# Head pairs and the dense experts' last norm of a one-layer decoder step: sums and spread moved between matmul groups, norm ahead of receptance, residual added on TensorE and moments taken by ScalarE

## Chip, core and metric

The kernel runs on one core of a Trainium2 chip, as one program. The time is the device time of one execution in microseconds (us), median over runs.

## The reference, cut to what matters

One layer of a decoder over 1024 prompt tokens and 8 single-token samples: an input projection, window attention beside an RWKV-7 time mix, a merge with layer norm, and a retrieval over 16,384 one-neuron experts with a second layer norm. The change touches two places. In the time mix:

```
kk = hs(k * k_k)                                                   # per head of 64
kk = kk * lax.rsqrt(jnp.maximum(jnp.sum(kk * kk, -1, keepdims=True), 1e-24))
k = k * (1.0 + (a - 1.0) * k_a)
bonus = (jnp.sum(hs(r * k * r_k), -1, keepdims=True) * hs(v))
```

And in the last step, where `peer` is the expert sum and `layer_norm` takes mean and mean squared deviation over 1024 features with an epsilon of 1e-5:

```
y = layer_norm(DEEPNORM_ALPHA * h + peer(h, ...), ln2_g, ln2_b)
```

## The kernel before

The trunk runs twice. The early part (`e_` tiles) holds 256 prompt tokens and the 8 samples, 264 columns in one column group (`NG` = 1). The late part (`l_` tiles) holds 768 tokens in two column groups of 384 (`NG` = 2). In each part `project_pairs` loops over the 8 pairs of heads. The engines run their own programs in program order and meet at semaphores whose counts come from the three lists `PE`, `AC` and `DV` (`Steps`). Layout: features of a pair on the 128 partitions, tokens along the free axis.

A turn of the loop (pair p) on TensorE: the two small products w and a (L776), g (L776), the projection r (L770, 8 weight tiles for each column group), the sums of squares per head (L797, one 128-token run after another, into `sums`), the projection v, the spread of the reciprocal norm over 64 partitions (L805, into `rb`), the bonus product (L776, of `rk`), in the early part three transposes (L813), the projection k of the next pair, and in the early part six more transposes (L825, `dec_t`). All three projections write the same PSUM tile `zp[0]`, so v waits until ScalarE has copied r out, and k until v is out. w of the next pair waits for `bonus_done`, since the bonus product and w share `zp[1]`; g waits until ScalarE has made tanh of w (L856).

On VectorE a turn is: fk, kkr, sq (the squares), the decay and its scan, ta and kp, a block of background work, the clamp (L969), fr and rk (L947, L973), the reciprocal (L977), kk and kka (L980, L981), a second background block, fv and bonus (L947, L991), the four products alpha, beta, kappa, rho (L995), dend, betae and kappae (L998), and in the early part two copies of the transposes (L1003, L1004).

The background work (`Rows`, `bg.dve`) is there in the late part only: GpSimd fetches expert rows by index into a ring, VectorE takes dot products (L440), adds weighted rows (L457) and does selection steps. `beside["pair"]` gives each block 4 slots (four dots, or four adds with a selection step) in pairs 0, 2, 4 and 6, 8 slots in pairs 1, 3 and 5, none in pair 7. ScalarE copies and scales each projection, then takes the square root of the clamped norm and the exponentials, and at the end of a turn applies Gelu to the dots. SyncE loads weights and stores results; in a turn it stores the gate, fv and the bonus, then the six products. An early turn and a late turn are numbered 0 to 7 below.

`experts` is the last stage. Three blocks of 128 tokens (`ND` = 3) go densely through all experts in 16 chunks of 8 tiles: TensorE makes 8 tiles of scores (L2755, from `l_c_wo`, loaded as `u_cols`), ScalarE Gelu (L2773), VectorE the gate weight (L2796), and TensorE the 48 matmuls into `vps` (L2763). Beside it the rows of three more blocks are fetched and added by VectorE. After the last chunk and the last row, VectorE adds ALPHA times h to `vps` (L2812), takes moments (L465 to L467), and normalises (L472 to L474).

Of the kernel before, what the change touches and what calls it, by code (L numbers as in the profile page):

```python
# [14 lines left out]
P = 128  # L15
# [629 lines left out]
def project_pairs(nc, A, pt, bg, plan):  # L645
# [6 lines left out]
    PE = Steps("w", "a", "g", "r", "ss", "v", "rb", "bonus", *only("raw_t", "dec_t"))  # L652
    AC = Steps("w", "a", "g", "r", "r_s", "norm", "Dinv", "D", "Dprev", *only("wdec"), "v", "v_s", *only("raw_t"))
    DV = Steps("k_f", *only("k_fs"), "kkr", "sq", "lw", "scan", "lprev", "a", "ka1", "kp",
               "ssm", "r_f", *only("r_fs"), "rk", "rinv", "kk", "kka", "v_f", *only("v_fs"),
               "alpha", "beta", "kappa", "rho", "dend", "betae", "kappae", *only("dec_t0", "dec_t1"))
# [7 lines left out]
    with ExitStack() as ctx:  # L664
# [52 lines left out]
        def _(sp):  # L717
# [12 lines left out]
            def store(p):  # L730
# [3 lines left out]
                sp.wait_ge(dve_done, DV.after("v_f", p))  # L734
                sp.dma_start(A["rw"][p, R_V, :, tokens], fv[:, PROMPT]).then_inc(rw_out[R_V], 16)
                sp.wait_ge(bonus_done, p + 1)
                for here, there in pt.spans:
                    sp.dma_start(A["bonus"][p, :, there], bonus[:, here]).then_inc(b_out, 16)
                for name, i in (("alpha", R_ALPHA), ("beta", R_BETA), ("kappa", R_KAPPA), ("rho", R_RHO),
# [3 lines left out]
                    if name == "rho":  # L743
                        sp.wait_ge(dve_done, DV.after("dend", p))
                        sp.dma_start(A["dend"][p, :, pt.t0 // CL:pt.t0 // CL + NC], dend[:, :]).then_inc(d_out, 16)

# [19 lines left out]
        def _(pe):  # L766
            def project(q, s, done):
                for g in range(NG):
                    for k in range(KT):
                        mm = pe.matmul(zp[s][:, g, 0:GZ], w[q][:, k, :], xT[:, k, g * GZ:(g + 1) * GZ],  # L770
                                       start=(k == 0), stop=(k == KT - 1))
                mm.then_inc(done, 1)

# [8 lines left out]
            for p in range(NPAIR):  # L782
# [11 lines left out]
                project(Q_PAIR_R, 0, pe_done)  # L794
                pe.wait_ge(dve_done, DV.after("sq", p))
                for i, (o, m) in enumerate(runs):
                    mm = pe.matmul(sums[0:m, 2 * i:2 * i + 2], sq[:, o:o + m], bd[:, 0:P:HD], start=True, stop=True)  # L797
                mm.then_inc(pe_done, 1)
                pe.wait_ge(w_in[2], 16 * p + 16)
                pe.wait_ge(act_done, AC.after("r", p))  # L800
                project(Q_PAIR_V, 0, pe_done)
                pe.wait_ge(dve_done, DV.after("rinv", p))
                for i, (o, m) in enumerate(runs):
                    for h in range(2):
# [2215 lines left out]
```

## Time and profile before

| | |
|---|---|
| median of 3 runs | 4436.56 us (4434.66 to 4444.74) |
| profiled execution, its own time | 4439.95 us |
| span of the profile | 4438.0 us |
| TensorE busy | 3811.5 us (86%) |
| VectorE busy | 3042.0 us (69%) |
| ScalarE busy | 949.5 us (21%) |

The profile is one execution. A row of the timeline has the start in us from the span's start, the duration in us, engine, line, operation, output and inputs, shapes and the count of merged instructions; brackets hold the idle time of that engine just ahead and what ended it. One fp32 matmul of the source shows as two records. A busy share says little here, as each stage has its own limit: what counts is which wait ends last in the stage that changes.

### The profile page before, as it was taken

Reading aid. Unit: us, or ns where it says so; the run is one execution under the profiler, and the core shown is the slowest. Engines: PE = TensorE matmul, PEld = TensorE weight load, DVE = VectorE, ACT = ScalarE, POOL = GpSimd, SP = SyncE. Lnnn points to the kernel's source line nnn. Section 1 sums busy time; section 2 is a strip of 40 time slices with the busy share of each in tenths; the row PEclk is TensorE's granted clock in tenths of the full one; section 3 lists DMA queues with packets and bytes.
Section 4 is the critical chain, followed back from the end, with each engine's and each line's share of the span. In section 5 each row is a group of like instructions: output and inputs, shape, how many; then the busy total and the mean of one; then the engine's idle time right before and its main releaser. Section 6 shows DMA issues by size and latency. Waiting matters only on the chain. (4 is left out here: it accounts for less than half of the span.)

```text
span 4438.0 us, 71873 instructions
## 1 busy us (share of the span) xinstructions
PE 3811.5 (86%) x28123; PEld 2546.5 (57%) x28123; DVE 3042.0 (69%) x5972; ACT 949.5 (21%) x1985; POOL 1818.0 (41%) x1489
## 2 busy tenths in 40 slices
PE   7986788799988788888778886669999999999997
PEld 6766665555555477777665464554544444445443
DVE  0454432588588557777686478877888888977768
ACT  1341220110233222222351013770000000010000
POOL 0016000067133023333225207736666566666664
PEclk9997889899998898898679997669999999999998
DMA  7542353499576556765639643449999999999997
GB/s 172 162 155 91 111 182 142 151 360 403 188 258 233 198 197 215 249 219 188 212 125 381 244 157 48 99 145 404 407 398 393 405 403 398 384 405 407 404 406 285
DMA packets 434557, 1152.50 MB, mean 260 GB/s; under 512 B 80735, under 2 KB 175524, under 8 KB 430852
## 3 DMA queue, kind: packets, MB, share of 16 engines
q0 software_dynamic: 207216, 687.87, 42.8%
q1 hardware_dynamic: 194276, 419.98, 26.1%
q10 hardware_dynamic: 32727, 40.05, 2.6%
q8 instruction: 224, 3.67, 0.3%
q14 instruction: 114, 0.93, 0.1%
HBM read 1044.67 MB, written 113.65 MB: 261 GB/s over the span
## 5 line engine op out<-in xcount | busy, mean ns | idle before, releaser
L2755 PE MATMUL x_sps<-c_big,l_c_wo 128*128 128x384 f32 x2048 | 689.8, 499 | 80.1 <-DMA l_c_wo<-u_cols 70.1
L384 POOL DMA_INDIRECT l_w_ring<-u_rows,k_eidx x256 | 295.3, 1153 | 967.0 <-DVE l_w_dots L440 410.3
L2763 PE MATMUL x_vps<-l_c_v,x_w 128*128 128x512 f32 x1536 | 662.1, 592 | 1.6 <-DVE x_w L2796 1.6
L384 POOL DMA_INDIRECT w_ring<-u_rows,k_eidx x384 | 483.3, 1259 | 429.3 <-DVE w_dots L440 254.5
L2755 PEld LDWEIGHTS x_sps<-c_big,l_c_wo 128*128 128x128 f32 x2048 | 399.3, 196 | 371.1 <-DMA l_c_wo<-u_cols 78.1
L457 DVE SCALAR_TENSOR_TENSOR w_yacc<-w_ring,w_wts,w_yacc 128x1024 f32<-128x1024 f32 x384 | 493.4, 1285 | 63.3 <-DMA w_ring<-v_rows,k_eidx 49.1
L2763 PEld LDWEIGHTS x_vps<-l_c_v,x_w 128*128 128x128 f32 x1536 | 291.8, 190 | 365.9 <-issue 358.2
L440 DVE CUSTOM_DVE_ANT_0 w_ring<-w_ring,w_h 128x1024 f32<-128x1024 f32 x384 | 452.5, 1224 | 49.7 <-DMA w_h<-s_h 25.9
L384 POOL DMA_INDIRECT w_ring<-v_rows,k_eidx x384 | 423.6, 1103 | 130.5 <-issue 114.8
L384 POOL DMA_INDIRECT l_w_ring<-v_rows,k_eidx x256 | 290.2, 1133 | 316.7 <-DVE l_w_yacc L457 253.0
L457 DVE SCALAR_TENSOR_TENSOR l_w_yacc<-l_w_ring,l_w_wts,l_w_yacc 128x1024 f32<-128x1024 f32 x256 | 328.9, 1285 | 30.7 <-DMA l_w_ring<-v_rows,k_eidx 18.8
L580 PE MATMUL l_pzp<-c_big,l_c_w 128*128 128x384 f32 x960 | 313.0, 488 | 18.0 <-DMA l_c_w<-w_tiles 18.0
L440 DVE CUSTOM_DVE_ANT_0 l_w_ring<-l_w_ring,l_w_h 128x1024 f32<-128x1024 f32 x256 | 305.6, 1224 | 20.4 <-DMA l_w_ring<-u_rows,k_eidx 9.7
L2773 ACT ACTIVATE x_w<-x_sps 128x384 f32<-128x384 f32 x128 | 62.7, 490 | 1139.5 <-PE x_sps L2755 984.5
L580 PEld LDWEIGHTS l_pzp<-c_big,l_c_w 128*128 128x128 f32 x960 | 182.4, 190 | 148.2 <-DMA l_c_w<-w_tiles 18.3
L770 PE MATMUL l_qzp<-c_big,l_c_w 128*128 128x385 f32 x768 | 260.9, 498 | 4.2 <-PEq L144 4.2
L2370 POOL DMA_INDIRECT s_G<-l_f_at_gate,l_f_at_u x128 | 207.4, 1620 | 125.6 <-DVEq L2553 67.9
L770 PEld LDWEIGHTS l_qzp<-c_big,l_c_w 128*128 128x128 f32 x768 | 149.1, 195 | 111.8 <-issue 15.8
L2796 DVE TENSOR_TENSOR x_w<-x_w,l_c_wo 128x384 f32<-128x384 f32 x128 | 68.1, 558 | 154.1 <-ACT x_w L2773 151.9
L2320 PE MATMUL l_f_gps<-l_f_two,l_f_one 128*128 128x128 f32 x512 | 101.9, 361 | 75.0 <-ACT l_f_two L2428 67.2
L2320 PEld LDWEIGHTS l_f_gps<-l_f_two,l_f_one 128*128 128x128 f32 x512 | 87.9, 259 | 87.7 <-ACT l_f_two L2428 73.5
L580 PE MATMUL e_pzp<-c_big,e_c_w 128*128 128x264 f32 x480 | 116.8, 402 | 19.7 <-DMA e_c_w<-w_tiles 12.7
(642 smaller groups left out, 6170.1 us busy)
## 6 DMA issues: line engine op xcount, KB each, us to landing
l_c_wo<-u_cols SPq DMA_DIRECT2D x128, 512.0 KB
l_c_v<-v_rows SPq DMA_DIRECT2D x128, 512.0 KB
e_c_w<-w_tiles SPq DMA_DIRECT2D x54, 512.0 KB, 3.5
l_c_w<-w_tiles SPq DMA_DIRECT2D x54, 512.0 KB
l_c_wo<-s_G SPq DMA_DIRECT2D x16, 1536.0 KB
s_rw<-l_q_out SPq DMA_DIRECT2D x48, 384.0 KB
s_G<-l_f_stage ACTq DMA_DIRECT2D x8, 2048.0 KB
s_zT<-l_pz ACTq DMA_DIRECT2D x30, 384.0 KB
```

The source lines that it names most:

```text
L384: pool.indirect_dma_start(out=self.ring[:, r, :], out_offset=None, in_=self.A[table], in_offset=bass.IndirectOffsetOnAxis(ap=idx[:, s:s + ...
L440: V.tensor_tensor_reduce(ring[:, q % self.RING, :], ring[:, q % self.RING, :], self.h[b % self.HB][:, :], 1.0, 0.0, ALU.mult, ALU.add, sel ...
L457: self.mark(dve, V.scalar_tensor_tensor(ya[:, :], self.ring[:, q % self.RING, :], self.wts[:, s:s + 1], ya[:, :], ALU.mult, ALU.add), self ...
L580: mm = pe.matmul(zp[j][:, g, 0:GN], w[u % 3][:, k, :], xT[:, k, x0 + g * GN:x0 + (g + 1) * GN], start=(k == 0), stop=(k == KT - 1))
L770: mm = pe.matmul(zp[s][:, g, 0:GZ], w[q][:, k, :], xT[:, k, g * GZ:(g + 1) * GZ], start=(k == 0), stop=(k == KT - 1))
L2320: mm = pe.matmul(gps[q % 2][:, t * NKEY:(t + 1) * NKEY], one[q % 2][:, t, :], two[q % 2][:, t, :], start=True, stop=True)
L2370: pool.indirect_dma_start(out=matrix, out_offset=bass.IndirectOffsetOnAxis(ap=at_u[:, s:s + 1], axis=0), in_=gates[:, s:s + 1], in_offset= ...
L2755: mm = pe.matmul(sps[n % 2][:, 0:ND * P], u[n % 4][:, k, :], hT[:, k, :], start=(k == 0), stop=(k == KT - 1))
L2763: mm = pe.matmul(vps[k][:, x * 512:(x + 1) * 512], w[:, e, k * P:(k + 1) * P], v[:, e, x * 512:(x + 1) * 512], start=(c == 0 and e == 0), ...
L2773: act.activation(w[:, e, :], sps[n % 2][:, 0:ND * P], ACT.Gelu).then_inc(S["act_done"], 1)
L2796: V.tensor_tensor(w[:, e, :].rearrange("p (g t) -> p g t", t=TGW), w[:, e, :].rearrange("p (g t) -> p g t", t=TGW), G[:, :, e, :], ALU.mul ...
```

## The change

In `project_pairs` the orders change. With one column group the sums of squares stand ahead of projection r and the spread stays behind projection v. With two groups the sums stand between the two column groups of r and the spread between those of v. The clamp moves directly behind kp, ahead of the first background block, and the reciprocal directly behind that block, ahead of fr and rk; ScalarE's square root moves ahead of the copy of r. On VectorE the products alpha to kappae move ahead of fv and the bonus, and the second background block moves behind the bonus. The stores of fv and bonus move behind the six products in SyncE's program.

In `experts` six fp32 matmuls of ALPHA times the identity with h are put into the accumulation of `vps`, in the middle of the scores of the last chunk. VectorE's sum and moments are gone; ScalarE copies `vps` with a running sum, scales it to the negative mean, squares the deviation with a running sum and takes the root, for blocks 0 and 1 ahead of the last row block's own square root and for block 2 behind it.

```
-    PE = Steps("w", "a", "g", "r", "ss", "v", "rb", "bonus", *only("raw_t", "dec_t"))
+    PE = Steps("w", "a", "g", "ss", "r", *(("rb", "v") if pt.ng > 1 else ("v", "rb")), "bonus", *only("raw_t", "dec_t"))
...
-            def project(q, s, done):
+            def project(q, s, done, between=None):
+
                 for g in range(NG):
...
+                    if between is not None and g == 0 < NG - 1:
+                        between()
                 mm.then_inc(done, 1)
+                if between is not None and NG == 1:
+                    between()
+
+            def squares(p):
+                pe.wait_ge(dve_done, DV.after("sq", p))
...
+            def spread(p):
+                pe.wait_ge(dve_done, DV.after("rinv", p))
...
-                project(Q_PAIR_R, 0, pe_done)
-                pe.wait_ge(dve_done, DV.after("sq", p))
...
+                if NG == 1:
+                    squares(p)
+                project(Q_PAIR_R, 0, pe_done, None if NG == 1 else lambda: squares(p))
                 pe.wait_ge(w_in[2], 16 * p + 16)
                 pe.wait_ge(act_done, AC.after("r", p))
-                project(Q_PAIR_V, 0, pe_done)
-                pe.wait_ge(dve_done, DV.after("rinv", p))
...
+                project(Q_PAIR_V, 0, pe_done, lambda: spread(p))
                 pe.wait_ge(act_done, AC.after("g", p))
+                pe.wait_ge(dve_done, DV.after("rk", p))
                 small(1, bd[:, :], rk[:, :])
...
                 act.activation(pt.grouped(gate[:, :]), zp[1][:, :, 0:GN], ACT.Copy).then_inc(act_done, 1)
+                act.wait_ge(dve_done, DV.after("ssm", p))
...
                 do("kp", V.scalar_tensor_tensor(kp[:, :], kp[:, :], 1.0, fk[:, :], ALU.add, ALU.mult))
-                bg.dve(dve, 4 * fetched(p))
                 dve.wait_ge(pe_done, PE.after("ss", p))
...
                 do("ssm", ins)
...
+                bg.dve(dve, 4 * fetched(p))
                 dve.wait_ge(act_done, AC.after("norm", p))
...
                 do("kka", V.tensor_tensor(kka[:, :], kk[:, :], ta[:, :], ALU.mult))
-                bg.dve(dve, 4 * fetched(p))
-                dve.wait_ge(act_done, AC.after("v_s", p))
+                dve.wait_ge(act_done, AC.after("Dprev", p))
...
+                dve.wait_ge(act_done, AC.after("v_s", p))
+                mixed(2, fv, "v", C_MUV)
...
+                bg.dve(dve, 4 * fetched(p))
```

The last stage:

```
+                    if (c, e) == (NCH - 1, CH // 2):
+                        pe.wait_ge(S["ident_done"], 1)
+                        pe.wait_ge(S["acc_in"], 16 * ND)
+                        for k in range(ND):
+                            for x in range(2):
+                                pe.matmul(vps[k][:, x * 512:(x + 1) * 512], scaled_ident[:, :], acc[:, k, x * 512:(x + 1) * 512],
+                                          start=False, stop=False)
...
+            def moments(k):
+
+                one = slice(k, k + 1)
+                act.wait_ge(S["v_psum"], ND * (NCH - 1) + k + 1)
+                act.activation(acc[:, k, :], vps[k][:, :], ACT.Copy, accum_out=nm3[:, one]).then_inc(S["moments"], 1)
...
+                act.activation(nm3[:, one], nm3[:, one], ACT.Copy, scale=-1.0 / DM).then_inc(S["moments"], 1)
...
+                act.activation(u[k][:, :, :].rearrange("p a b -> p (a b)"), acc[:, k, :], ACT.Square, bias=nm3[:, one],
+                               accum_out=ss3[:, one]).then_inc(S["moments"], 1)
...
+                act.activation(rs3[:, one], ss3[:, one], ACT.Sqrt, bias=eps[:, :], scale=1.0 / DM).then_inc(S["std3"], 1)
...
+            rows.act(act, rows.NGT + 1 - rows.act_at)
+            act.wait_ge(S["eps_done"], 1)
+            for k in range(ND - 1):
+                moments(k)
             rows.act(act, rows.TOTAL)
...
+            moments(ND - 1)
...
-            dve.wait_ge(S["acc_in"], 16 * ND)
             for k in range(ND):
-                dve.wait_ge(S["v_psum"], ND * (NCH - 1) + k + 1)
-                mark(V.scalar_tensor_tensor(acc[:, k, :], acc[:, k, :], ALPHA, vps[k][:, :], ALU.mult, ALU.add), S["summed"], k + 1)
...
+                dve.wait_ge(S["std3"], k + 1)
+                lnk(V.reciprocal(rs3[:, one], rs3[:, one]))
```

TensorE's program in an early turn before the change: `e_qsums` are the sums of squares, `e_qrb` the spread, and the 8-row products into `e_qzp` are the projections r and v.

```order
L776 MATMUL e_qzp<-e_q_lora,e_q_up 128x264 x3
L770 MATMUL e_qzp<-c_big,e_c_w 128x264 x8
L797 MATMUL e_qsums<-c_bd,e_q_sq 128x2 x2
L797 MATMUL e_qsums<-c_bd,e_q_sq 8x2
L770 MATMUL e_qzp<-c_big,e_c_w 128x264 x8
L805 MATMUL e_qrb<-c_ident,e_q_norm 64x128 x4
```

The same place after the change:

```order
L795 MATMUL e_qzp<-e_q_lora,e_q_up 128x264 x3
L782 MATMUL e_qsums<-c_bd,e_q_sq 128x2 x2
L782 MATMUL e_qsums<-c_bd,e_q_sq 8x2
L771 MATMUL e_qzp<-c_big,e_c_w 128x264 x16
L789 MATMUL e_qrb<-c_ident,e_q_norm 64x128 x4
```

The sums of squares stood between the projections r and v; now they stand ahead of r, and r and v follow each other with nothing between.

TensorE's program in a late turn before the change, from w, a and g to the next pair's k:

```order
L776 MATMUL l_qzp<-l_q_lora,l_q_up 128x384 x6
L770 MATMUL l_qzp<-c_big,l_c_w 128x385 x16
L797 MATMUL l_qsums<-c_bd,l_q_sq 128x2 x6
L770 MATMUL l_qzp<-c_big,l_c_w 128x385 x16
L805 MATMUL l_qrb<-c_ident,l_q_norm 64x128 x12
L776 MATMUL l_qzp<-l_q_fk,c_bd 128x384 x2
L770 MATMUL l_qzp<-c_big,l_c_w 128x385 x16
```

And after it:

```order
L795 MATMUL l_qzp<-l_q_lora,l_q_up 128x384 x6
L771 MATMUL l_qzp<-c_big,l_c_w 128x385 x8
L782 MATMUL l_qsums<-c_bd,l_q_sq 128x2 x6
L771 MATMUL l_qzp<-c_big,l_c_w 128x385 x16
L789 MATMUL l_qrb<-c_ident,l_q_norm 64x128 x12
L771 MATMUL l_qzp<-c_big,l_c_w 128x385 x8
L795 MATMUL l_qzp<-l_q_fk,c_bd 128x384 x2
L771 MATMUL l_qzp<-c_big,l_c_w 128x385 x16
```

The sums moved into the middle of r and the spread into the middle of v; the second group of r and the first of v now stand side by side.

VectorE's program in an early turn before the change, from kka (L981) on: fv, bonus, the products, the two copies.

```order
L981 TENSOR_TENSOR e_q_ta<-e_q_kk,e_q_ta 128x264
L947 SCALAR_TENSOR_TENSOR e_q_fv<-e_qz,e_q_prm,e_q_fv 128x256
L949 SCALAR_TENSOR_TENSOR e_q_fv<-e_q_sh,e_q_prm,e_q_fv 128x8
L991 TENSOR_TENSOR e_q_bonus<-e_qzp,e_q_fv 128x264
L995 TENSOR_TENSOR e_q_out<-e_q_kk,e_q_lprev 128x256
L995 TENSOR_TENSOR e_q_out<-e_q_ta,e_q_Di 128x256
L995 TENSOR_TENSOR e_q_out<-e_q_kp,e_q_Di 128x256
L995 TENSOR_TENSOR e_q_out<-e_q_fr,e_q_lcum 128x256
L996 COPY e_q_dend<-e_q_lcum 128x4
L998 TENSOR_TENSOR e_q_out<-e_q_out,e_q_dend 128x256 x2
L1003 COPY e_q_decn<-e_qtp 8x512
```

And after it:

```order
L992 TENSOR_TENSOR e_q_ta<-e_q_kk,e_q_ta 128x264
L1000 TENSOR_TENSOR e_q_out<-e_q_kk,e_q_lprev 128x256
L1000 TENSOR_TENSOR e_q_out<-e_q_ta,e_q_Di 128x256
L1000 TENSOR_TENSOR e_q_out<-e_q_kp,e_q_Di 128x256
L1000 TENSOR_TENSOR e_q_out<-e_q_fr,e_q_lcum 128x256
L1001 COPY e_q_dend<-e_q_lcum 128x4
L1003 TENSOR_TENSOR e_q_out<-e_q_out,e_q_dend 128x256 x2
L959 SCALAR_TENSOR_TENSOR e_q_fv<-e_qz,e_q_prm,e_q_fv 128x256
L961 SCALAR_TENSOR_TENSOR e_q_fv<-e_q_sh,e_q_prm,e_q_fv 128x8
L1009 TENSOR_TENSOR e_q_bonus<-e_qzp,e_q_fv 128x264
L1015 COPY e_q_decn<-e_qtp 8x512
```

fv and the bonus moved behind the seven products and dend; the late turn has the same order, with the second background block behind the bonus.

## Rows read from the trace of the kernel before

**Rows 1.** Page, 40 slices: busy tenths of the DMA engines

```profile
DMA  7542353499576556765639643449999999999997
```

**Rows 2.** Timeline, an early turn, TensorE

```profile
194.94 3.72 PE L770 MATMUL e_qzp<-c_big,e_c_w 128*128 128x264 f32 x16
...
198.50 0.63 PE L797 MATMUL e_qsums<-c_bd,e_q_sq 128*128 128x2 f32 x6
...
199.24 3.80 PE L770 MATMUL e_qzp<-c_big,e_c_w 128*128 128x264 f32 x16
...
202.97 0.87 PE L805 MATMUL e_qrb<-c_ident,e_q_norm 128*64 128x128 f32 x12
...
208.21 0.27 PE L825 MATMUL e_qtp<-c_ident,e_q_fr 128*8 128x128 f32 x1
```

**Rows 3.** Timeline, the same turn, VectorE

```profile
193.28 0.68 DVE L1003 COPY e_q_decn<-e_qtp 8x512 f32<-8x512 f32 x1 [0.15 <-PE e_qtp L825]
...
195.61 0.43 DVE L955 TENSOR_TENSOR e_q_sq<-e_q_kkr 128x264 f32<-128x264 f32 x1
...
205.70 0.43 DVE L991 TENSOR_TENSOR e_q_bonus<-e_qzp,e_q_fv 128x264 f32<-128x264 f32 x1
...
208.08 0.88 DVE L998 TENSOR_TENSOR e_q_out<-e_q_out,e_q_dend 128x256 f32<-128x256 f32 x2
...
209.12 0.68 DVE L1003 COPY e_q_decn<-e_qtp 8x512 f32<-8x512 f32 x1 [0.15 <-PE e_qtp L825]
```

**Rows 4.** Timeline, late turns, TensorE

```profile
1161.22 6.58 PE L776 MATMUL l_qzp<-l_q_lora,l_q_up 64*128 64x384 f32 x12 [2.01 <-issue]
...
1207.95 1.56 PE L776 MATMUL l_qzp<-l_q_lora,l_q_up 128*128 128x384 f32 x4 [1.81 <-ACT l_q_tw L856]
...
1254.23 2.94 PE L776 MATMUL l_qzp<-l_q_lora,l_q_up 64*128 64x384 f32 x8 [5.44 <-DVE l_q_bonus L991]
...
1259.51 10.51 PE L770 MATMUL l_qzp<-c_big,l_c_w 128*128 128x385 f32 x32
...
1271.12 10.60 PE L770 MATMUL l_qzp<-c_big,l_c_w 128*128 128x385 f32 x32
...
1284.50 10.51 PE L770 MATMUL l_qzp<-c_big,l_c_w 128*128 128x385 f32 x32
1297.62 2.16 PE L776 MATMUL l_qzp<-l_q_lora,l_q_up 64*128 64x384 f32 x8 [2.61 <-DVE l_q_bonus L991]
1300.69 2.93 PE L776 MATMUL l_qzp<-l_q_lora,l_q_up 128*128 128x384 f32 x4 [0.91 <-ACT l_q_tw L856]
```

**Rows 5.** Timeline, late turns, ScalarE

```profile
1203.71 0.81 ACT L845 ACTIVATE l_qz<-l_qzp 128x770 f32<-128x770 f32 x1 [11.43 <-PE l_qzp L770]
...
1205.61 1.28 ACT L394 ACT_TABLE_LOAD   x1
```

**Rows 6.** Timeline, late turns, VectorE

```profile
1218.50 1.22 DVE L440 CUSTOM_DVE_ANT_0 l_w_ring<-l_w_ring,l_w_h 128x1024 f32<-128x1024 f32 x1
...
1231.43 0.17 DVE L969 TENSOR_SCALAR l_q_norm<-l_qsums 128x12 f32<-128x12 f32 x1
...
1524.36 1.95 DVE L998 TENSOR_TENSOR l_q_out<-l_q_out,l_q_dend 128x768 f32<-128x768 f32 x2
```

**Rows 7.** Timeline, last chunk of the experts stage, TensorE

```profile
4321.47 20.80 PE L2755 MATMUL x_sps<-c_big,l_c_wo 128*128 128x384 f32 x64
...
4348.30 23.42 PE L2755 MATMUL x_sps<-c_big,l_c_wo 128*128 128x384 f32 x64 [6.03 <-DMA l_c_wo<-u_cols]
4371.55 41.36 PE L2763 MATMUL x_vps<-l_c_v,x_w 128*128 128x512 f32 x96
```

**Rows 8.** Timeline, last chunk and end, VectorE

```profile
4361.95 0.56 DVE L2796 TENSOR_TENSOR x_w<-x_w,l_c_wo 128x384 f32<-128x384 f32 x1 [3.75 <-ACT x_w L2773]
...
4415.01 1.22 DVE L2812 SCALAR_TENSOR_TENSOR x_acc<-x_acc,x_vps 128x1024 f32<-128x1024 f32 x1
...
4424.44 0.16 DVE L472 RECIPROCAL x_rs<-x_rs 128x1 f32<-128x1 f32 x1
```

More of the change, by code:

```diff
@@ L745, in store @@
                         sp.dma_start(A["dend"][p, :, pt.t0 // CL:pt.t0 // CL + NC], dend[:, :]).then_inc(d_out, 16)
+                sp.wait_ge(dve_done, DV.after("v_f", p))
+                sp.dma_start(A["rw"][p, R_V, :, tokens], fv[:, PROMPT]).then_inc(rw_out[R_V], 16)
+                sp.wait_ge(bonus_done, p + 1)
+                for here, there in pt.spans:
+                    sp.dma_start(A["bonus"][p, :, there], bonus[:, here]).then_inc(b_out, 16)
             load_up(0)
@@ L771, in project @@
                                        start=(k == 0), stop=(k == KT - 1))
+                    if between is not None and g == 0 < NG - 1:
+                        between()
                 mm.then_inc(done, 1)
+                if between is not None and NG == 1:
+                    between()
+            def squares(p):
+                pe.wait_ge(dve_done, DV.after("sq", p))
+                for i, (o, m) in enumerate(runs):
+                    mm = pe.matmul(sums[0:m, 2 * i:2 * i + 2], sq[:, o:o + m], bd[:, 0:P:HD], start=True, stop=True)
+                mm.then_inc(pe_done, 1)
+            def spread(p):
+                pe.wait_ge(dve_done, DV.after("rinv", p))
+                for i, (o, m) in enumerate(runs):
+                    for h in range(2):
+                        mm = pe.matmul(rb[h * HD:(h + 1) * HD, o // GN, o % GN:o % GN + m], norm[0:m, 2 * i + h:2 * i + h + 1].broadcast_to([m, HD]),
+                                       ident[0:m, 0:m], start=True, stop=True)
+                mm.then_inc(pe_done, 1)
             def small(s, lhsT, rhs):
@@ L864, in _ @@
                 act.activation(pt.grouped(gate[:, :]), zp[1][:, :, 0:GN], ACT.Copy).then_inc(act_done, 1)
+                act.wait_ge(dve_done, DV.after("ssm", p))
+                for i, (rows, cols) in enumerate(whole):
+                    ins = act.activation(norm[rows, cols], norm[rows, cols], ACT.Sqrt)
+                ins.then_inc(act_done, 1)
                 act.wait_ge(pe_done, PE.after("r", p))
@@ L874, in _ @@
                     shift(Q_PAIR_R, p)
-                act.wait_ge(dve_done, DV.after("ssm", p))
-                for i, (rows, cols) in enumerate(whole):
-                    ins = act.activation(norm[rows, cols], norm[rows, cols], ACT.Sqrt)
-                ins.then_inc(act_done, 1)
                 act.activation(Di[:, :], lcum[:, :], ACT.Exp, scale=-1.0).then_inc(act_done, 1)
@@ L2808, in _ @@
             rows.dve(dve, 8 * rows.TOTAL)
[L2809 removed]
             for k in range(ND):
[L2811 to L2815 removed]
+                one = slice(k, k + 1)
+                dve.wait_ge(S["std3"], k + 1)
+                lnk(V.reciprocal(rs3[:, one], rs3[:, one]))
+                lnk(V.scalar_tensor_tensor(acc[:, k, :], acc[:, k, :], nm3[:, one], rows.ln[:, 0, :], ALU.add, ALU.mult))
+                mark(V.scalar_tensor_tensor(acc[:, k, :], acc[:, k, :], rs3[:, one], rows.ln[:, 1, :], ALU.mult, ALU.add),
+                     S["acc_done"], k + 1)
 def program(nc, A, phases=99):
```

49 lines of the change are left out of this document (18 added, 31 removed).

## The prediction

> **What bounds the kernel now.** I read the page first, then the timeline of the stages that change, engine by engine, then the waits there. On the page the reader is to see the DMA engines full through the last nine slices but the very end [rows 1]: in the experts stage the loads set the pace, so time gained ahead of it shifts it whole, and only its last 60 us can be won inside it. The change touches three stages, each with its own limit, and the sum is one term for each.
>
> Early turns (one column group). TensorE is nearly always at work. A turn lasts 209.12 - 193.28 = 15.84 us [rows 3]. The sums (0.63 us) run between r and v, and v starts at 199.24, a tenth of a microsecond after they end: in that time ScalarE copies r out of PSUM, so the sums cost nothing there [rows 2].
>
> Late turns (two groups). TensorE and VectorE hold each other up. TensorE waits 5.44 us and 2.61 us at the start of a turn for the bonus, which VectorE makes only after its second background block [rows 4]. The stage lasts from 1161.22 [rows 4] to 1524.36 + 1.95 = 1526.31 [rows 6], 365.1 us.
>
> The end. VectorE starts the dense tail at 4415.01 and reaches the first reciprocal at 4424.44 [rows 8]. TensorE is done at 4371.55 + 41.36 = 4412.9 [rows 7]. So the last thing that bounds is VectorE's own queue.
>
> **Early turns: a loss.** The sums now stand ahead of r and wait for sq. In the rows sq ends at 195.61 + 0.43 = 196.04 [rows 3], while r began at 194.94 [rows 2]. VectorE cannot be earlier: sq is behind the two copies, and these wait for TensorE's transposes. So TensorE waits until about 196.15, does the sums (0.63 us, some 0.1 more since its weight loads are no longer hidden), and starts r at 196.9: 1.9 us late. From r to v nothing is won back, since ScalarE's copy, not the sums, sets the 4.30 us between their starts. Second, the transposes of `dec_t` wait for fv, now behind the products. VectorE's products end at 208.08 + 0.88 = 208.96; with the bonus (0.4) moved behind fv, fv ends near 208.6 and the transposes start near 208.8 in place of 208.21 [rows 2, 3]: 0.55 us. A turn gets 15.84 + 1.9 + 0.55 = 18.3 us. Seven full turns give 7 x 2.45 = 17, the first wait is half as long since VectorE has no copies ahead of it, and the last turn keeps only the 0.55: together **+18.5 us**. Bounds: +13 (the wait halved, as if sq came 0.8 us sooner) and +22 (all weight loads of the sums exposed and a semaphore's delay at each of three hand-overs). The square root ahead of the copy of r costs nothing here, as the clamp is free before r's 3.6 us end; if it were late, v would be.
>
> **Late turns: a gain.** With the second background block behind the bonus, w never waits, if VectorE gets kk to bonus done within the projection k. The new turn on TensorE, from the end of one k to the next:
> - to the start of g: 4.35 us. In the turn at 1203.6 (ScalarE's copy begins at 1203.71) g starts at 1207.95, held by tanh, which stands behind the copy, the scaling, a table load of 1.28 and a Gelu [rows 4, 5];
> - g, then r with the sums in the middle: 1.39 (taken off the start of r at 1259.51 and the row of g, 1.56 with overlap) and 1271.12 - 1259.51 = 11.61 [rows 4];
> - new: v waits for the copy of r, no longer covered by the sums: 0.81 [rows 5] and two hand-overs, 1.2 us;
> - v with the spread, and the bonus product: 1284.50 - 1271.12 = 13.38 [rows 4]; k: 10.5 [rows 4].
>
> That is 42.4 us. The background blocks that stay on this path: the first one now stands between clamp and reciprocal, and the spread needs the reciprocal 23.8 us into the turn. In pairs 1, 3 and 5 the block is two groups long, 1231.43 - 1218.50 = 12.93 us [rows 6]. The clamp comes when the sums are done, at 12.4, so the reciprocal is there at 25.7: a wait of 1.9 us, and another 1.3 for a spread at the lower clock, 45.7 us. Pair 3 has a block some 2 us longer by its selection steps (my estimate), 47.6; pair 5 a shorter one, no wait. In the one-group pairs the reciprocal is there in time. After a two-group turn VectorE starts its next turn 6 to 8 us late, which moves kp and with it clamp and root to 14 to 16.5, just ahead of the end of r at 17.4: if that were more, ScalarE's copy of r would be queued behind the root, and v behind it.
>
> Sum: turn 0 takes 43.4, turns 1 and 3 45.7 and 47.6, four turns 42.4, and the last ends with VectorE's bonus near 37.7 (it has no k): 344. Against 365.1 this is **-21 us**. Bounds: -7 (next part) and -30 (no wait and no gap at all).
>
> **A rule on ScalarE's table loads.** The row shows 1.28 us for the load, and g started 1207.95 - 1205.61 = 2.34 us after the load did [rows 4, 5]. A tanh of 768 columns, which by the copy's row takes 0.8 to 0.9, and a Gelu of four columns are in these 2.34, so nothing else is. The Trainium skill, page "ScalarE: Activation LUTs", section "What ACT_TABLE_LOAD costs", gives each switch a drain of about 1.38 us on top. By that an estimate from the page would put 1.4 us more into each of seven late turns and the late gain at 11 us instead of 21; the rows show no such drain, so I go by them.
>
> **The end: a gain.** VectorE loses L2812 to L467 for three blocks: 4424.44 - 4415.01 = 9.43 us [rows 8]. It keeps the reciprocal and two passes for each. ScalarE's new work is four steps of at most 1.1 us for each block (770 columns take 0.81 [rows 5], so 1024 take near 1.05): the third block starts when TensorE is done and is ready 3 us later, 4416; VectorE needs it 5.7 us after its start. TensorE's six extra matmuls cost 41.36 / 48 x 6 = 5.2 us [rows 7] and are put where it waits 6.03 us for a tile of `u_cols` [rows 7]: hidden. If that wait were gone they would put TensorE 5.2 us later and cost VectorE some 3. They may give more: behind the wait, four tiles took 23.42 us, where the four ahead took 20.80 [rows 7], so a busy TensorE saves 2.6, and VectorE waits 3.75 us for ScalarE in that stretch [rows 8]. The end gives **-12 us**, between -6 and -12.5.
>
> The other pieces cost nothing: the scaled identity and epsilon are made at the stage's start; h is loaded as before; in SyncE's program the store of fv and bonus moves behind six stores, and all are issued before the next pair's k is done.
>
> **Sum.** +18.5 - 21 - 12 = -14.5 on 4439.95 us of the profiled execution, which stands 3.4 above the median. On the median: 4422, and with a little of the clock case below, **4423**.
>
> **The rivals.**
> - *The clock drops in the late turns.* A wait of 1.8 us ahead of g left it at full rate (1.56), but after 2.61 + 0.91 us of idle g took 2.93 us [rows 4], which is 1.2 in place of 2.4 GHz. The new turn idles 1.8 ahead of g and 1.2 ahead of v, on either side of that. If each of six turns loses the 1.4 us in g and near 1 us in the first matmuls of r (my estimate), the late gain is 7, and the total -0.5: 4436. The Trainium skill, page "TensorE: Matmul & The Clock Gate", section "Why this matters for your kernels", warns of idle gaps between bursts of matmuls for this reason. Chance 0.2.
> - *Slower: the early turns lose the clock as well.* TensorE now idles twice in a turn of 18 us, 1.1 ahead of the sums and 0.7 ahead of v. If all of r (3.6 us) ran at half rate in each turn, 8 x 3.6 = 29 us are added: 4452. It ends above no change from about 3 us a turn. For it speaks the row at 2.93, against it that today's early turns idle about as often, in shorter pieces. Chance 0.1.
> - *The late turns gain their whole idle time*, as the copies out of PSUM overlap better than I have them: -30, total 4413. Chance 0.1.
> - *The extra matmuls do not fit the wait*, because the tile lands sooner: the end gives 6, total 4428. Chance 0.1.
>
> **How the numbers follow.** My forecast has 0.5, with its own range of 4416 to 4430. A measurement of this kernel tells about 0.2% (9 us) from no change, so faster means below 4427.7. Of the forecast 0.45 lies there, all of the third rival and half of the fourth: 0.6. Same gets 0.3, slower 0.1. The range 4408 to 4442 leaves out most of the second rival and the fringes.
>
> **What would show it.** In the profile after: early turns of 18.3 us with TensorE waiting for sq ahead of L782, and the pause between r and v still 0.7; late turns of 42 to 43 us without a wait for the bonus, 2 to 4 us of wait for the reciprocal in pairs 1 and 3 only; six L2768 matmuls inside the wait near 4342 and no wait of 6 us left; VectorE going from the last row's norm straight into reciprocals without a stall. The prediction is wrong if early turns stay at 16 us, if late turns show g near 2.9 throughout, or if VectorE waits for ScalarE at the end.

## The result, and the profile after the change

The changed kernel takes 4448.13 us (median of 20 runs, 4431.67 to 4464.11) against 4435.87 us for the kernel before (20 runs, 4427.53 to 4444.74): the ratio is 1.0027, with a 95% interval of 1.0017 to 1.0037. It is slower by some 12 us, where a gain of 12 to 14 us (4423) was forecast. The profiled execution after has 4456.54 us and a span of 4454.7.

The early turns, TensorE's timeline, to hold against [rows 2]:

```profile
199.64 0.71 PE L795 MATMUL e_qzp<-e_q_lora,e_q_up 128*128 128x264 f32 x2 [0.56 <-ACT e_q_tw L868]
201.38 0.70 PE L782 MATMUL e_qsums<-c_bd,e_q_sq 128*128 128x2 f32 x6 [1.03 <-DVE e_q_sq L967]
202.02 5.51 PE L771 MATMUL e_qzp<-c_big,e_c_w 128*128 128x264 f32 x16
208.10 3.80 PE L771 MATMUL e_qzp<-c_big,e_c_w 128*128 128x264 f32 x16 [0.57 <-ACT e_qz L882]
...
221.38 0.70 PE L782 MATMUL e_qsums<-c_bd,e_q_sq 128*128 128x2 f32 x6 [1.03 <-DVE e_q_sq L967]
222.01 3.83 PE L771 MATMUL e_qzp<-c_big,e_c_w 128*128 128x264 f32 x16
226.41 3.80 PE L771 MATMUL e_qzp<-c_big,e_c_w 128*128 128x264 f32 x16 [0.57 <-ACT e_qz L882]
...
240.32 5.49 PE L771 MATMUL e_qzp<-c_big,e_c_w 128*128 128x264 f32 x16
```

The wait for sq and the pause ahead of v are there as forecast. But r (16 records) takes 3.83 us in two of the seven full turns and 5.5 in the other five: from r at 222.01 to r at 240.32 are 18.31 us, the 18.3 of the forecast, and from r at 202.02 to r at 222.01 are 19.99. The granted clock tells them apart: as a share of 2.4 GHz it is 1.00 from 222.01 to 225.84 and 0.69 from 202.02 to 207.53, so a part of these matmuls ran at 1.2 GHz and the rest at 2.4. Before, r took 3.72 us in each full turn, as in [rows 2]. The windows of 165 to 293 us show it over the whole stretch, before and then after (busy time by engine, then PEclk, 0.98 and 0.93):

```profile
165.00:293.00 128.00, 115.01 (x635) 89.68 (x633) 86.88 (x238) 65.29 (x139) 13.51 (x24) 0.98 0.53 166
```

```profile
165.00:293.00 128.00, 112.18 (x548) 83.09 (x547) 71.42 (x193) 56.07 (x118) 10.42 (x19) 0.93 0.47 146
```

The late turns, TensorE after the change, from one w to the next, to hold against [rows 4]:

```profile
1228.93 2.53 PE L795 MATMUL l_qzp<-l_q_lora,l_q_up 64*128 64x384 f32 x8
1233.27 2.67 PE L795 MATMUL l_qzp<-l_q_lora,l_q_up 128*128 128x384 f32 x4 [1.81 <-ACT l_q_tw L868]
1235.73 5.97 PE L771 MATMUL l_qzp<-c_big,l_c_w 128*128 128x385 f32 x16
...
1249.21 5.41 PE L771 MATMUL l_qzp<-c_big,l_c_w 128*128 128x385 f32 x16 [0.99 <-ACT l_qz L882]
1256.47 1.53 PE L789 MATMUL l_qrb<-c_ident,l_q_norm 128*64 128x128 f32 x24 [1.84 <-issue]
...
1274.94 1.56 PE L795 MATMUL l_qzp<-l_q_lora,l_q_up 64*128 64x384 f32 x4
```

No turn waits for the bonus any more. The waits that are left up to the last turn are those forecast: 1.8 or 1.9 ahead of g, 1.0 ahead of v, and in pair 1 a wait of 1.84 ahead of the spread (3.6 in pair 3, as the run "late part and end" below shows in its own rows). What was not counted is g at 2.67 in place of 1.56, and the first half of r at 5.97 in place of 5.34: together 8.64 us in place of 6.90, and the other turns of this trace with a slow g have much the same, 8.55 to 8.64. Nor was a wait of 3.43 us ahead of g in the last turn, which the kernel before has too (3.44). From 1185.54 to VectorE's last bonus at 1536.4 the stage has 350.8 us, not 344, against 365.1.

The end, TensorE and then VectorE after the change, to hold against [rows 7, 8]:

```profile
4351.25 20.80 PE L2775 MATMUL x_sps<-c_big,l_c_wo 128*128 128x384 f32 x64
4371.89 5.31 PE L2768 MATMUL x_vps<-x_acc,x_scaled_ident 128*128 128x512 f32 x12
4377.04 20.80 PE L2775 MATMUL x_sps<-c_big,l_c_wo 128*128 128x384 f32 x64
4397.68 41.36 PE L2783 MATMUL x_vps<-l_c_v,x_w 128*128 128x512 f32 x96
```

```profile
4439.75 1.28 DVE L474 SCALAR_TENSOR_TENSOR w_yacc<-w_yacc,w_rs,w_ln 128x1024 f32<-128x1024 f32 x1
4441.07 0.17 DVE L2849 RECIPROCAL x_rs<-x_rs 128x1 f32<-128x1 f32 x1
4441.27 1.28 DVE L2850 SCALAR_TENSOR_TENSOR x_acc<-x_acc,x_nm,w_ln 128x1024 f32<-128x1024 f32 x1
```

The six extra matmuls are L2768. VectorE goes from the last row's norm into the first reciprocal without a stall. From its arrival at the dense tail to the end of the span are 4454.7 - 4441.07 = 13.6 us; before they were 4438.0 - 4415.01 = 23.0 [rows 8]. That is the forecast's 9.4, and in each of the nine traces with the new end these last steps take 13.6 us. TensorE shows no wait for `u_cols` here, so the six extra matmuls stand in the open with 5.3 us, but TensorE is done at 4439.0, ahead of VectorE.

### The profile page after: what moved, and what is told of

The parts are those of the page before. It is cut to its first block and busy times, and to the rows that moved or that the text cites. A ratio compares the mean times of both kernels' runs of the same rounds, so it can differ in the third digit from the quotient of the medians.

```text
span 4454.7 us, 71922 instructions
## 1 busy us (share of the span) xinstructions
PE 3838.5 (86%) x28135; PEld 2563.1 (58%) x28135; DVE 3034.9 (68%) x5958; ACT 958.4 (22%) x2001; POOL 1827.2 (41%) x1489
```

## Experiments

Each run is told with its ratio to the kernel before on the same chip. Chips differ (medians of before from 4404 to 4439 us), so only ratios and lengths of stages are compared. "Early part" is the stretch from the first matmul of the early pairs to the first of the scan behind them, "late part" the same for the late pairs, each from the starts that the traces show. Line numbers differ between the kernels.

### One part at a time

**The end alone.** `project_pairs` as before, the experts stage as changed.

> The kernel before with only the change at the end of the experts stage. By the theory read from the two traces the end gives what it gives in the changed kernel: from VectorE's arrival at the dense tail to the end of the span 13.6 us in place of 23.0, and the whole kernel about 9 to 12 us faster (ratio near 0.9975). Rival: the gain is given back ahead of the tail, because the six extra matmuls put TensorE later or the trace's 9.4 us was luck of one execution: then the time is within 4 us of before.

Measured: ratio 0.9991 (0.9980 to 1.0002). From VectorE's first dense reciprocal at 4377.39 to the end of the span (4391.0) again 13.6 us. The timing alone does not tell the gain from nothing. Over the traces of all kernels here, the first experts matmul to the end of the span took 1443.6 us in the mean of nine without the new end (1439.0 to 1448.1) and 1434.7 in nine with it (1429.4 to 1439.1): 8.9 us less.

**The pairs, in the early part alone and in the late part alone.** The experts stage is as before. Both forms of the function stand in the file, as `project_pairs_0` (before) and `project_pairs_1` (changed), and one is chosen by the number of column groups; for the late part alone the names are exchanged:

```
 def project_pairs(nc, A, pt, bg, plan):
+    one = project_pairs_1 if pt.ng == 1 else project_pairs_0
+    one(nc, A, pt, bg, plan)
```

> The kernel before with the pair change only where there is one column group (the early part). By the theory that the early turns lost 27 us in the changed kernel (exposed sums and the wait for v some 13, the wait for fv some 6, r at the lower clock some 9) the whole kernel is 25 to 30 us slower (ratio near 1.0061), the first e_r_ps matmul that reads e_c_powers is 27 us later, and what follows is shifted by the same amount with no growth. Rival: a loss at the start also costs the later stages (the changed kernel was a further 14 us later between the late turns and the last expert chunks): then 35 to 45 us slower. Second rival, my forecast's size of this term: 18.5 us slower.

Measured: 1.0068 (1.0048 to 1.0088), 30 us slower; the early part 178.3 us against 150.4 in the end-only kernel on that chip.

> The kernel before with the pair change only where there are two column groups (the late part). By the trace of the changed kernel the late turns give 14 us, so 14 us faster (ratio near 0.9968) if nothing behind them changes. Rival: the scan, attention and experts stages behind the late turns lose 12 to 14 us as a consequence of the late change (the trace of the changed kernel lost them there): then within 4 us of before. Second rival: the forecast's 21 us.

Measured: 0.9971 (0.9958 to 0.9985), 13 us faster; the late part 379.5 us against 390.9. It keeps its gain.

**Late part and end, early part as before.**

> The changed kernel with the early part as it was before: pair change in the late part, dense residual and statistics at the end. If the parts add up and the early part is what costs: 14 plus 9 to 12, so 23 to 26 us faster than before (ratio near 0.9945), faster than both kernels. If the later stages lose because of the late change: only 9 to 12 us faster. If the early part's 27 us were partly made up for by slack elsewhere, less than 12 + 27 = 39 us would lie between this and the changed kernel.

Measured: 0.9955 (0.9939 to 0.9971), 20 us faster. The three parts add up: +30 - 13 - 4 = +13, where the whole change has +12; each of the three has an interval of 5 to 9 us to either side. So the early part alone turned a gain into a loss. TensorE's rows of g and of the spread in the late turns of this kernel, each with the wait ahead of it in brackets, show the clock come and go:

```profile
1200.66 2.59 PE L1173 MATMUL l_qzp<-l_q_lora,l_q_up 128*128 128x384 f32 x4 [1.81 <-ACT l_q_tw L1246]
...
1223.86 1.53 PE L1167 MATMUL l_qrb<-c_ident,l_q_norm 128*64 128x128 f32 x24 [1.85 <-DVE l_q_norm L1363]
...
1246.77 1.56 PE L1173 MATMUL l_qzp<-l_q_lora,l_q_up 128*128 128x384 f32 x4 [1.91 <-ACT l_q_tw L1246]
...
1314.12 2.83 PE L1167 MATMUL l_qrb<-c_ident,l_q_norm 128*64 128x128 f32 x24 [3.61 <-DVE l_q_norm L1363]
...
1338.42 2.93 PE L1173 MATMUL l_qzp<-l_q_lora,l_q_up 128*128 128x384 f32 x4 [1.91 <-ACT l_q_tw L1246]
```

The same wait of 1.9 us is followed by g at 1.56 in one turn and at 2.93 in another.

### What costs in the early turns

All three have the early change alone, with one thing in it altered.

**fv and the bonus back ahead of the products.**

```
-               "alpha", "beta", ..., "kappae", "v_f", *only("v_fs"), ...
+               "v_f", *only("v_fs"), "alpha", "beta", ..., "kappae", ...
```

> The pair change in the early part only, with fv and the bonus back ahead of the products; the sums stay ahead of r and the products, clamp and root as in the change. By the theory that the dec_t transposes waited 0.7 to 0.9 us a turn for fv behind the products, the early part is 5 to 6 us shorter than with the whole early change, and the kernel some 24 us slower than before (with the early change alone it was 30 slower). Rival: dec_t was never what set the next turn, so the time stays at +30; or the next turn's sq gets later because VectorE has more ahead of it, and the waiting moves there. In the trace: no wait left ahead of the dec_t transposes.

Measured: 1.0055 (1.0037 to 1.0072), 24 us; early part 171.1, so 7 less than 178.3, of which 1.7 are one turn fewer with r at 5.51 (four of seven, not five). Both theories have something: the wait ahead of the `dec_t` transposes is gone in all turns but the last, and TensorE, earlier at the sums, waits a little longer there. One turn and the next:

```profile
181.30 0.70 PE L1160 MATMUL e_qsums<-c_bd,e_q_sq 128*128 128x2 f32 x6 [1.52 <-DVE e_q_sq L1345]
181.94 5.51 PE L1149 MATMUL e_qzp<-c_big,e_c_w 128*128 128x264 f32 x16
...
200.82 0.70 PE L1160 MATMUL e_qsums<-c_bd,e_q_sq 128*128 128x2 f32 x6 [1.08 <-DVE e_q_sq L1345]
201.45 3.83 PE L1149 MATMUL e_qzp<-c_big,e_c_w 128*128 128x264 f32 x16
```

**Sums and root back behind r.**

```
-                if NG == 1:
-                    squares(p)
-                project(Q_PAIR_R, 0, pe_done, ...)
+                project(Q_PAIR_R, 0, pe_done)
+                squares(p)
```

> The pair change in the early part only, with the sums back between r and v and the root back behind ScalarE's copy and scaling of r; fv stays behind the products. By the theory that the sums' place costs both the exposed wait for sq (some 13 us over the stage, with the wait ahead of v) and the drop of the clock in r (9 us in the trace of the changed kernel, 5.5 us in place of 3.7 in five of seven turns), only the 6 us of the dec_t wait are left: 6 to 8 us slower than before. Rival: the clock drops because of the longer wait ahead of the transposes and not because of the wait for sq: then r stays at 5.5 us in most turns and the kernel is 15 us slower.

Measured: 1.0003 (0.9987 to 1.0020), 3 us slower in the medians, which does not tell it from before; early part 155.8. The rival falls: with a wait of 0.37 still ahead of the transposes and 0.56 ahead of g, r is at full rate in each of the seven full turns.

```profile
193.22 0.27 PE L1214 MATMUL e_qtp<-c_ident,e_q_fr 128*8 128x128 f32 x1 [0.37 <-DVE e_q_fv L1338]
...
195.79 3.72 PE L1149 MATMUL e_qzp<-c_big,e_c_w 128*128 128x264 f32 x16
199.35 0.63 PE L1160 MATMUL e_qsums<-c_bd,e_q_sq 128*128 128x2 f32 x6
200.09 3.80 PE L1149 MATMUL e_qzp<-c_big,e_c_w 128*128 128x264 f32 x16
```

**The waits filled with work.**

```
+            def fill(count):
+                for _ in range(count):
+                    pe.matmul(dump[:, 0:256], bd[:, :], xT[:, 0, 0:256], start=True, stop=True)
...
+                    fill(3)
                     squares(p)
...
+                    fill(1)
                 pe.wait_ge(act_done, AC.after("r", p))
```

> The pair change in the early part only, with three matmuls of 256 columns into an unused bank of PSUM ahead of the wait for sq and one ahead of the wait for the copy of r in each turn, so that TensorE is busy in most of its two waits; nobody reads their result. If the idle time ahead of the sums is what takes the clock, r lasts 3.8 us in every turn and the kernel is 9 to 12 us faster than with the early change alone, some 20 slower than before. Rival: the clock follows something else (the 0.2 us matmuls of the sums and transposes, the mean load of the stage): r stays at 5.5 us in most turns, and the kernel is 30 us slower or more, since three matmuls at the lower clock (2.3 us) no longer fit the wait.

Measured: 1.0057 (1.0038 to 1.0076), 23 to 25 us slower, in place of 30; early part 168.7, which is 10 less than with the early change alone and 19.0 more than the mean of 149.7 in three traces of before. The times alone would not tell this from the early change; the length of the early part does. Order and waits are the same, only idle time ahead of the sums and of v was replaced, and r is back at 3.83 in every turn:

```profile
198.17 1.46 PE L1160 MATMUL e_qdump<-c_big,c_bd 128*128 128x256 f32 x6
199.46 0.63 PE L1165 MATMUL e_qsums<-c_bd,e_q_sq 128*128 128x2 f32 x6
200.02 3.83 PE L1150 MATMUL e_qzp<-c_big,e_c_w 128*128 128x264 f32 x16
203.68 0.59 PE L1160 MATMUL e_qdump<-c_big,c_bd 128*128 128x256 f32 x2
204.33 3.83 PE L1150 MATMUL e_qzp<-c_big,e_c_w 128*128 128x264 f32 x16
```

A turn has 218.29 - 200.02 = 18.27 us from r to r. The window of 165 to 293 us in this kernel has PEclk 1.00:

```profile
165.00:293.00 128.00, 120.75 (x638) 92.52 (x637) 79.18 (x212) 59.53 (x124) 11.84 (x21) 1.00 0.50 157
```

### What costs in the late turns

All three have the early part as before and the new end.

**The waits ahead of g and v filled.**

```
+                fill(4)
                 pe.wait_ge(act_done, AC.after("w", p))
                 small(1, up[:, 1, :], lora[1][:, :])
...
+                fill(2)
                 pe.wait_ge(act_done, AC.after("r", p))
```

> Late pair change and the end, early part as before (the e4 version), with four matmuls of 256 columns into an unused bank of PSUM ahead of TensorE's wait for the tanh of w and two ahead of its wait for the copy of r, in each late turn; nobody reads their result. In e4 five of the late turns ran g at 2.3 to 2.9 us in place of 1.56 and the first sixteen matmuls of r longer than 5.3. If the idle 1.8 to 1.9 us ahead of g take the clock, g is 1.6 in every turn, the stage from the first projection to the scan's first matmul falls from 379.4 to 370 us or less, and the kernel is 28 to 30 us faster than before. Rival: the clock falls for another reason (the load over a longer stretch, or the waits for the reciprocal in pairs 1 and 3), then g stays at 2.3 to 2.9 and the stage at 379, or longer, since four matmuls at half rate (3 us) do not fit the wait.

Measured: 0.9918 (0.9895 to 0.9941), 36 us faster than before; late part 370.8, which is 8.6 less than in the version without filling. The two timings lie 16 us apart, but they come from two chips and their intervals touch, so the other 7 are not shown to be a gain. g is 1.56 in each of the last seven turns, where the version without filling has 2.3 to 2.9 in five of them. The waits ahead of the spread are not filled: in pair 3 one of 3.76 us is still followed by matmuls at the lower clock, 6.80 us in place of 5.44. In the first turn TensorE has no wait ahead of g: there the four take 3.6 us, and the turn has 45.0 us in place of 43.5.

```profile
1205.75 1.99 PE L1160 MATMUL l_qdump<-c_big,c_bd 128*128 128x256 f32 x8
1207.63 1.56 PE L1178 MATMUL l_qzp<-l_q_lora,l_q_up 128*128 128x384 f32 x4
1209.02 5.34 PE L1150 MATMUL l_qzp<-c_big,l_c_w 128*128 128x385 f32 x16
```

**The background block split around the reciprocal.**

```
-                bg.dve(dve, 4 * fetched(p))
+                bg.dve(dve, 4 if fetched(p) else 0)
...
                 do("rinv", ins)
+                bg.dve(dve, 4 * (fetched(p) - 1) if fetched(p) else 0)
```

> The e4 version with VectorE's background block between clamp and reciprocal split in the late part: one group's half ahead of the reciprocal, the other behind it, so that the reciprocal is there when v's first half is done also in pairs 1, 3 and 5. By the theory that TensorE's waits of 1.8 and 3.6 us ahead of the spread in pairs 1 and 3, with the spread at the lower clock behind them, are part of what the late turns cost, the stage is 6 to 7 us shorter (373 us) and no such wait is left. Rival: the wait moves to the next turn's w, because the bonus comes no sooner and TensorE arrives earlier there: then the stage is within 2 us of 379.

Measured: 0.9934 (0.9907 to 0.9960), late part 380.1. My theory fell, and the rival's size came true in another place than it said. The waits ahead of the spread are gone, but the stage has gained nothing: in pair 4 a new wait stands ahead of the sums, and the matmuls behind it are slow (8.06 us in place of 5.42).

```profile
1346.49 2.22 PE L1160 MATMUL l_qsums<-c_bd,l_q_sq 128*128 128x2 f32 x12 [1.94 <-DVE l_q_sq L1345]
1348.57 8.06 PE L1149 MATMUL l_qzp<-c_big,l_c_w 128*128 128x385 f32 x16
```

**Both.**

> Both of the two edits above together. If the two costs are separate they add up: some 15 us less than 379.4 in the late stage, the kernel 33 to 36 us faster than before. Rival: with both waits gone the bonus of VectorE becomes the bound in the two-group pairs, and less than 10 us are gained.

Measured: 0.9925 (0.9904 to 0.9946), late part 370.9, so 8.5 us less than 379.4 and not 15: the split adds nothing to the filling. The rival holds in kind, but what bounds is sq, not the bonus. Behind pair 3's second block VectorE is late for sq by 3.69 us; the six turns from the second w to the last have 42.3, 42.9, 42.3, 49.7, 42.3 and 42.4 us:

```profile
1199.28 2.53 PE L1178 MATMUL l_qzp<-l_q_lora,l_q_up 64*128 64x384 f32 x8
...
1241.62 2.53 PE L1178 MATMUL l_qzp<-l_q_lora,l_q_up 64*128 64x384 f32 x8
...
1341.66 2.32 PE L1165 MATMUL l_qsums<-c_bd,l_q_sq 128*128 128x2 f32 x12 [3.69 <-DVE l_q_sq L1354]
```

### Does the forecast's sum come true with the clock kept?

**The whole change, with the waits filled in both parts.**

> The changed kernel whole, with the filling matmuls in both parts: three ahead of the wait for sq and one ahead of v in each early turn, four ahead of g and two ahead of v in each late turn. My forecast had 14.5 us of gain, and the runs so far put its failure down to the clock, which it counted at nothing. If that is all of it, this kernel, with all of the change's waits but no idle time that takes the clock, does what was forecast for the change: early +18.6, late -20.4, end -9.4, so some 11 us faster than before (ratio near 0.9975), against +12 for the change as it was. Rival: a loss behind the late turns that belongs to the change whatever the clock does (7 to 14 us in the first traces): then 0 to 3 us slower than before.

Measured: 0.9975 (0.9962 to 0.9988), 11 us faster than before. Early part 168.4 (+18.7 on before's 149.7), late part 367.6. The 3.2 us by which its late part is shorter than with the filling alone lie in the first turn, 42.0 us in place of 45.0, where the four matmuls ahead of g take 2.0 us and not 3.6.

### Stages behind the pairs

In the first two traces the changed kernel lost a further 15 us between the late pairs and the experts stage, 11.4 of them in the late scan. Before and the changed kernel were traced twice more each, on several chips.

> The kernel before once more, for a trace from this chip. The stages of the changed kernel behind the late turns were 14 us longer than before in the first two traces, though their code is the same. If that is a spread between executions or chips, the scan of the late part (602 us in the first trace, 613 in the changed kernel's) is as long here as in the other traces of this chip, whichever kernel it is (568 to 577 in the four so far). If the pair change costs it, the scan here is as short as in the end-only run (568) and longer in the runs with a pair change.

> The changed kernel once more, for a second trace. If the 14 us that it lost behind the late turns against the kernel before are a property of the change, its scan of the late part is 10 us longer than that of the other kernels of this call, and the last expert chunk starts later by as much. If they are a spread between executions, it is not. Early turns: again 18.3 us where r lasts 3.8 and 20.0 where it lasts 5.5, the first e_r_ps matmul near 326.

> A third trace of the changed kernel, on the same chip as the next run's. If the change costs the scan of the late part something, it is 8 to 11 us longer here than in the next run (613.6 and 611.5 us in the two traces so far, 602.2 and 603.5 in those of before, but on different chips); if not, within the 6 us by which kernels of one chip differed.

> A third trace of the kernel before, to be held beside the run above: the scan of the late part, the stretch from the late pairs to the first experts matmul, and from there to the end.

> The early change alone once more, for its stages behind the early part on the same chip as the two runs above. Early part 25 to 28 us longer than before's; r at 5.5 us in five or six of the turns. If the scan of the late part is as long as in the run of before, the early change costs nothing further on.

Measured, first to last start of `l_r_ps` matmuls, the late scan: before 602.2, 603.5 and 607.2 us; changed 613.6, 611.5 and 606.4; the early change alone 606.6. The last of before, of changed and the early one are from one chip, and there they agree within 0.8 us. On the chip of the first four experiments this stage took 568.5 (end alone) to 577.0 us, and on that of the next three, with before, 595.7 to 607.8. So the length of this scan differs between chips and executions by as much as the changed kernel's first trace was longer, and no run shows that this is part of the change's price. The early part repeats: 177.0, 177.5 and 178.3 us in the changed kernel. The late part repeats less well: 376.7, 379.7 and 384.7, with more or fewer slow turns.

## Why the prediction was wrong

**Where the terms came out.** With before's mean of three traces as the base (early part 149.7, late part 391.2), the changed kernel's three traces have 177.6 and 380.4.

| term | forecast | clock kept by filling | as changed |
|---|---|---|---|
| early part | +18.5 | +18.7, +19.0 | +27.9 |
| late part | -21 | -20.4 (last run: -23.6) | -10.8 |
| end | -12 | | -8.9 |
| sum | -14.5 | timed: -11 | +8.2; timed: +12 |

**The step that failed** is the rule by which I put the clock into rivals: "against it that today's early turns idle about as often, in shorter pieces", and for the late turns that 1.8 us ahead of g "left it at full rate". Each took what had happened behind a few gaps for a property of the gap. The clock was counted at nothing in both sums; it costs 9 us in the early part (27.9 less 18.7 to 19.0) and some 10 in the late one (9 to 13 by the traces compared). The filled waits show it: same order, same waits, little idle time, and the early terms came out within 1 us of the forecast, the late ones at -20.4 and -23.6 against -21. Of the 26 us between forecast and measurement, 19 are the clock and 3 the end; 4 stand in no stage. The trace of before already held the warning for the late turns: of its seven g behind the first turn, five take 2.77 to 2.93 us, and [rows 4] have one of them. Two more:

```profile
1354.85 2.93 PE L776 MATMUL l_qzp<-l_q_lora,l_q_up 128*128 128x384 f32 x4 [0.94 <-ACT l_q_tw L856]
1489.41 2.77 PE L776 MATMUL l_qzp<-l_q_lora,l_q_up 128*128 128x384 f32 x4 [3.44 <-ACT l_q_tw L856]
```

So the late change even raised the clock: from the second w to the last it is 0.92 before, 0.97 after and 0.99 with the waits filled. But the forecast took it as full.

Both clock rivals were right in mechanism and too high in price: r lost 1.7 us in five of seven full turns (in each of three traces of the changed kernel), not 3.6 in all eight, and the late gain fell by 10, not by 14. But they have one cause, and I gave the case that both come true no chance of its own: by their prices it would be some 4465, and it ends at +8 by the stages, on the slower side. That the second rival's 4452 is near the measured 4448 is chance: its early loss was three times too large, and the loss in the late part and at the end was not in it. None of the signs that I named for being wrong came up: turns of 18 us, g between 1.56 and 2.93, no stall at the end. The Trainium skill, page "TensorE: Matmul & The Clock Gate", section "Why this matters for your kernels", warns of idle gaps between bursts of matmuls. These traces agree in both parts, by 5.51 in place of 3.83 us in r and 2.67 in place of 1.56 in g, but behind gaps shorter than those that the page warns of, and there the measurement decides.

**Early turns**, apart from that: the wait of 1.1 to 1.2 us ahead of the sums measured 1.03, the 0.7 ahead of v 0.57 and the 0.55 for `dec_t` 0.53 a turn (16.37 in place of 15.84 us with sums and root behind r). A turn with r at full rate has the 18.3 us forecast. With sums and root behind r, 6.1 us of the early part's loss remain, the price of fv behind the products.

**Late turns**: the turn of 42.4 us is there, 42.3 where nothing waits and the clock is kept. Waits of 1.84 and 3.6 ahead of the spread in pairs 1 and 3 stand where they were forecast (1.9 and about 4). The last turn has 39.0 us, not 37.7; its wait ahead of g is 3.43 us and not 1.8. Each turn holds one table load of 1.28 us, so the rule of the Trainium skill on which the late gain would have been 11 (page "ScalarE: Activation LUTs", section "What ACT_TABLE_LOAD costs") would have made it 43.8. The late gain did come out at 11, but for another reason: the rows of ScalarE after the change have the load at its 1.28 and the next operation right behind it, with no drain between. Here the measurement decides against the page.

```profile
1230.93 1.28 ACT L394 ACT_TABLE_LOAD   x1
1232.22 0.20 ACT L394 ACTIVATE l_w_dots<-l_w_dots 128x4 f32<-128x4 f32 x1
1232.34 0.88 ACT L868 ACTIVATE l_q_tw<-l_qzp,l_q_hc 128x768 f32<-128x768 f32 x1
```

**The end**: 9.43 us of removed work was right to a tenth. The other 2.6 was not there. I read it from a stretch in which TensorE had waited 6.03 us for `u_cols`; of the nine traces without the new end two have such a wait in the last chunk (6.03 and 6.56), one has 0.49 and six have none. VectorE does not depend on it: in the traces of before it arrives at its tail 1420.1 and 1420.7 us after the first experts matmul with that wait, and 1421.4 without. So the 6 us of cover for the six matmuls was chance too. It cost nothing that the traces show, as TensorE still ends 2 us ahead of VectorE's arrival.

**A reading of [rows 1]** was off too: the DMA engines are full in the twelve slices ahead of the last, not in nine. No term of the sum used the count.

**Left open**: what decides that one wait of 1.03 us is followed by r at 3.83 and the next by 5.51. The stages add up to 8 where the timing says 12, with an interval of 7.5 to 16.4; that rest is within the spread and has no cause that these runs show.

## What to carry to other kernels

An order that lets TensorE wait in a place where it was busy costs twice: the wait, and the matmuls behind it at a lower clock. Price both before moving work ahead of a stall, and take a row where the clock survived a gap as one case, not as a rule. Where the waits can't be removed, a few matmuls that nobody reads can be cheaper than idling: with them the version with the early part left as it was is at 0.9918 (0.9895 to 0.9941) of the kernel before, the best measured here, though its interval overlaps with those of the two versions with the block split. Where there is no wait to fill, as in the first turn, the filling is work in the open, 2.0 to 3.6 us of it. An edit that helps the two-group part by giving TensorE less to wait for is not the same edit in the one-group part, where VectorE's sq came 1.03 us too late in each turn: try such a change on each shape apart.

## What the runs showed of the hardware that was not expected

After pauses of 0.56 and 1.03 us, with 0.7 us of work between them, sixteen matmuls took 5.51 us in most turns and 3.83 in others; with the pause of 1.03 filled, and that of 0.57 ahead of v, 3.83 in all. Pauses of 0.37 and 0.56 alone left them at 3.72. An activation that also gives a sum has a second row behind it, as ScalarE's rows of the third dense block show (start, length):

```profile
4440.46 1.15 ACT L2797 ACTIVATE l_c_wo<-x_acc,x_nm 128x1024 f32<-128x1024 f32 x1
4441.52 0.19 ACT L2797 ACTIVATION_READ_ACCUMULATOR l_c_wo<-x_acc,x_nm 128x1 f32 x1
4441.74 0.29 ACT L2800 ACTIVATE x_rs<-x_ss,x_eps 128x1 f32<-128x1 f32 x1
```

The row of 1.15 us is followed 1.28 us after its start, and an activation without a sum, of 0.81 at 1229.04, is followed after 0.84: so the sum costs some 0.1. And one and the same scan took 568 to 577 us on one chip and 596 to 614 in the other traces; why is not shown.
